# Chunk stage of a two-layer decoder step: both quarter steps behind one block, head norm weights in the rotation tables, and low halves ahead of rotations

## The chip, the cores and the metric

One core of a Trainium2 chip runs one inference step of a two-layer decoder trunk. The metric is the device time of the whole launch in microseconds, the median of three runs: 1617.29 us (1616.27 to 1617.42). The difference between two kernels is judged by medians on the same chip.

## What is computed

512 prompt tokens and 8 x 4 decode tokens (544 columns) pass two layers with shared weights for both groups. The part that the change touches is the first projection of each layer and what directly follows it for the sparse attention:

```python
a = rmsnorm(h, g_attn)
qa, ka, va, qi, ki, wi, qb, kb, vb, u = split_columns(a @ w_in)
qa = rope(rmsnorm(qa.reshape(B, T, N_HEADS_A, HEAD_DIM), g_q_a), pos)   # 6 heads of 64
ka = rope(rmsnorm(ka.reshape(B, T, N_KV_A, HEAD_DIM), g_k_a), pos)      # 2 heads of 64
qi = rope(qi.reshape(B, T, N_IDX_HEADS, IDX_DIM), pos)                  # 4 heads, no norm
ki = rope(ki[:, :, None, :], pos)[:, :, 0]
# rope: concatenate([x1*cos - x2*sin, x2*cos + x1*sin])
```

Behind it stand the selection of keys by the indexer, sparse attention, stick-breaking attention, a pooling mixer, the output projection, a convolutional FFN and a gated per-layer embedding. All of it is float32. Each large product is made from a high and a low half of both factors, three matmuls for one (`tri_product`).

## The kernel before, in words

The weights come in units of 1024 columns by 128 partitions, 106 per layer. A unit is loaded by SyncE into one of four buffers `w_raw` (`load_unit`, L519), ScalarE copies its high half to `w_H` (`split`, L892; the copy is recorded at L890) and VectorE subtracts to get its low half `w_L` (`split`, L1266, recorded at L1270). `w_H` and `w_L` have two buffers each, so the halves of unit u wait until TensorE has used unit u - 2 (`w_used`). VectorE's step raises `w_lo`, for which TensorE waits.

The chunk stage is the first in each layer. It has three chunks c (512, 452 and 384 columns of `w_in`, tokens as rows) of eight blocks k over the contraction; a unit holds two blocks, so chunk c uses the units 4c to 4c + 3. A block is four token tiles of three matmuls. The 32 decode tokens don't go through the tri-product there. `decode_step` (L1785) multiplies them in plain float32 with the unhalved weights in `w_raw`: step 0 takes the blocks 0 to 3 and stands behind k = 3, step 1 takes the blocks 4 to 7 and stands behind k = 5. The four quarters of the partitions hold partial sums, which ScalarE copies to `q_part` (`part_copy`, L980) and one matmul behind k = 7 adds (L1827). Each step raises `q_dec`. SyncE's loads of units 4 to 15 wait for it, since they overwrite what the steps read: units 4 and 5 for the first step, 6 and 7 for the second, and so on, 12 and 13 for the fifth.

From chunk 0 come the queries and keys of the sparse attention. ScalarE copies them out of PSUM with the token norm (`leave`, L960). VectorE makes the squares of the heads (`head_squares`, L1302), ScalarE the inverse roots (`inverse`), GpSimd multiplies each tile by its root (recorded at L728), waits for itself, and multiplies it by the norm weights of queries and keys (L731, L732), which raises `qk_ok`. VectorE rotates (`qk`, L1338, by `rotate`, L1315): three products with the tables of `dcon` and two additions into `r_tok` per tile, which raise `rope_ok`. TensorE transposes a tile (`turn`, L1757), ScalarE copies it to `featT` (`turned`, L952). The indexer's five heads from chunk 1 go the same way without a norm (`index` on VectorE, L1344).

The order on each engine is written out by hand, and an engine that waits holds all that stands behind it. Around the change it is:

- TensorE, c1: blocks 0 to 3, step 0, blocks 4 and 5, step 1, `turn(0, 0)`, blocks 6 and 7, sum, `turn(0, 1)`. c2: `turn(0, 2)`, `(0, 3)`, `(0, 4)`, `(1, 0)` ... `(1, 4)`, one behind each block, with the steps behind k = 3 and k = 5.
- ScalarE: split 4, `part_copy(0)`, `leave(0, 0..4)`, split 5, inverse roots, splits 6 and 7, `turned(0, 0)`, split 8, `part_copy(1)`, `turned(0, 1)`, `leave(1, 0..2)`, split 9, `turned(0, 2)`, `leave(1, 3)`, `turned(0, 3)`, `leave(1, 4)`, split 10, ..., `turned(1, 2)`, split 12, `part_copy(2)`, ...
- VectorE: split 4, `head_squares(0..2)`, split 5, `head_squares(3..4)`, split 6, `qk(0)`, split 7, `qk(1)`, split 8, `qk(2)`, `qk(3)`, split 9, `qk(4)`, `index(0)`, split 10, `index(1)`, split 11, `index(2)`, `index(3)`, split 12, `index(4)`, split 13.

Of the kernel before, what the change touches and what calls it, by code (L numbers as in the profile page):

```python
# [20 lines left out]
F32 = mybir.dt.float32  # L21
# [3 lines left out]
ALU = mybir.AluOpType  # L25
# [3 lines left out]
P = 128  # L29
# [41 lines left out]

C_ID, C_NTRI, C_NONE, C_ONE, C_INVW, C_INV16, C_EPS, C_1, C_SUM = 0, 128, 256, 384, 512, 514, 546, 547, 548
NC = 580
ACT_STEPS, DVE_STEPS, POOL_STEPS = 12, 157, 16
D_COS, D_SIN, D_MA = 0, 320, 640
ND = 928
M_REP, M_NEW = 2 * P, 4 * P
# [67 lines left out]
def build(nc, t_in, t_out):  # L145
    ctx = ExitStack()
    with ctx:
        def sb(name, shape, dt=F32, where=None):
            return (where or ctx).enter_context(nc.sbuf_tensor(name, shape, dt))
# [59 lines left out]
        raw_q = ExitStack()  # L209
        sb("raw_skip2", [P, 7336], F32, raw_q)  # L210
        q_part = sb("q_part", [P, 512], F32, raw_q)
        raw_q.close()
        stick = ExitStack()
        LW = 1280
# [151 lines left out]
        def hold(eng):  # L366


            eng.sem_inc(held, 1)
# [307 lines left out]
        def _(pool):  # L677
            for l in range(LAYERS):
# [39 lines left out]
                pool.memset(u_p[:, :, 0:15], 0.0).then_inc(u_zero, 1)  # L718
                pool.wait_ge(lay_ld, at(lay_ld, 6 * 16))
                hold(pool)  # L720
                pool.tensor_scalar(gains[:, 0, :], gains[:, 0, :], 0.125, None, ALU.mult)
                pool.wait_ge(hs_rec, at(hs_rec, 1))
                hold(pool)
                for t in range(TILES):
                    n = TOKW[t]
                    pool.wait_ge(p_ev, at(p_ev, t + 1))
                    x = x_tok[0:n, t, :].rearrange("p (h d) -> p h d", d=HD)
                    pool.tensor_tensor(x, x, hstat[0:n, t, :].unsqueeze(2).to_broadcast([n, 8, HD]), ALU.mult).then_inc(pool_step, steps.step())  # L728
                    pool.wait_ge(pool_step, steps.value())
                    hold(pool)  # L730
                    pool.tensor_tensor(x[:, 0:6, :], x[:, 0:6, :], gains[0:n, 0, :].unsqueeze(1).to_broadcast([n, 6, HD]), ALU.mult)  # L731
                    pool.tensor_tensor(x[:, 6:8, :], x[:, 6:8, :], gains[0:n, 1, :].unsqueeze(1).to_broadcast([n, 2, HD]), ALU.mult).then_inc(qk_ok, 1)  # L732
                for t in range(TILES):
                    pool.wait_ge(rope_ok, at(rope_ok, t + 1))
                    hold(pool)
# [504 lines left out]
        def _(dve):  # L1240
# [18 lines left out]
            for l in range(LAYERS):  # L1259
# [55 lines left out]
                def rotate(t, heads, parts):  # L1315

                    n = TOKW[t]
                    w = heads * HD
                    if (heads, t) != (8, 0):
                        dve.wait_ge(rope_ok, at(rope_ok, t if heads == 8 else 5 + t))  # L1320
                    x = x_tok[0:n, t, 0:w].rearrange("p (h d) -> p h d", d=HD)
                    cs = dcon[0:n, D_COS + 64 * t:D_COS + 64 * t + 64].unsqueeze(1).to_broadcast([n, heads, HD])
                    sn = dcon[0:n, D_SIN + 64 * t:D_SIN + 64 * t + 64].unsqueeze(1)
                    a = t1[0:n, 0:w].rearrange("p (h d) -> p h d", d=HD)
                    b = t2[0:n, 0:w].rearrange("p (h d) -> p h d", d=HD)
                    dve.tensor_tensor(a, x, cs, ALU.mult)
                    dve.tensor_tensor(b[:, :, 0:32], x[:, :, 32:64], sn[:, :, 0:32].to_broadcast([n, heads, 32]), ALU.mult)
                    dve.tensor_tensor(b[:, :, 32:64], x[:, :, 0:32], sn[:, :, 32:64].to_broadcast([n, heads, 32]), ALU.mult).then_inc(dve_step, steps.step())
                    dve.wait_ge(dve_step, steps.value())
                    for out, a0, a1, order in parts:  # L1330
                        i0, i1 = t1[0:n, a0:a1], t2[0:n, a0:a1]
                        if order:
                            i0, i1 = (v.rearrange("p (n j d) -> p n j d", n=2, j=3) for v in (i0, i1))
                            out = out.rearrange("p (j n d) -> p n j d", n=2, j=3)
                        ins = dve.tensor_tensor(out, i0, i1, ALU.add)
                    ins.then_inc(rope_ok, 1)

                def qk(t):  # L1338

                    n = TOKW[t]  # L1340
                    dve.wait_ge(qk_ok, at(qk_ok, t + 1))
                    rotate(t, 8, [(r_tok[0:n, t, 0:384], 0, 384, True), (r_tok[0:n, t, 384:512], 384, 512, False)])
# [67 lines left out]
                head_squares(3)  # L1410
                head_squares(4)
                split(6)
                qk(0)
                split(7)
                qk(1)
                split(8)
                qk(2)
                qk(3)
                split(9)
                qk(4)  # L1420
                index(0)
                split(10)
# [271 lines left out]
        def _(pe):  # L1694
# [12 lines left out]
            for l in range(LAYERS):  # L1707
                def at(s, n):

                    return l * per_layer[s.name] + n  # L1710
# [74 lines left out]
                def decode_step(c, step):  # L1785
# [4 lines left out]
                    elif step == 0:  # L1790
                        pe.wait_ge(p_ev, at(p_ev, i - 6))
                    if step:
                        pe.wait_ge(w_lo, at(w_lo, RAW + 4 * c + 3 + 1))
                    for j in range(4):
                        k = 4 * step + j
                        raw = w_raw[raw_slot(l, 4 * c + k // 2)]
# [4 lines left out]
                for c in range(3):  # L1801
                    w = CHUNK[c][1] - CHUNK[c][0]
                    for k in range(KD):
# [6 lines left out]
                        for t in range(TILES - 1):  # L1810
# [9 lines left out]
                            mm = tri_product(ps[0:n, i % 7, 0:w], aH[:, k, tok], aL[:, k, tok], wh, wl, k == 0, k == KD - 1)  # L1820
                            if k == KD - 1:
                                mm.then_inc(p_mm, 1)
                        if k in (3, 5):
                            decode_step(c, (k - 3) // 2)
                        if k == KD - 1:
                            pe.wait_ge(q_cp, at(q_cp, c + 1))
                            mm = pe.matmul(ps[0:TS, (5 * c + 4) % 7, 0:w], con[:, C_SUM:C_SUM + TS], q_part[:, 0:w], start=True, stop=True)  # L1827
# [4 lines left out]
                        if c == 1 and k == 1:  # L1832
# [3 lines left out]
                            for m in range(2):  # L1836
                                mm = pe.transpose(ps[:, 7, P * m:P * m + 120], pst_tok[0:120, P * m:P * m + P], ident[0:120, 0:120])
                            mm.then_inc(u_tr, 1)
                        if c == 1 and k in (5, 7):
                            turn(0, (k - 5) // 2)  # L1840
                        if c == 2:
                            turn(*((0, k + 2) if k < 3 else (1, k - 3)))

# [463 lines left out]
```

## Time and profile before

| | |
|---|---|
| median of three runs | 1617.29 us (1616.27 to 1617.42) |
| the profiled execution | 1620.47 us, its span 1618.7 us |
| mean granted clock of TensorE | 0.984 |
| TensorE busy with matmuls | 1556.1 us, 96% |
| VectorE, ScalarE, GpSimd busy | 883.4, 683.5, 276.4 us |
| chain that ended last | TensorE 79%, VectorE 13%, ScalarE 3% |
| chunk stage, first layer | about 20.9 to 105.3 us |
| chunk stage, second layer | about 812 to 897.2 us |

The page gives the shares of each engine and the chain of waits, the timelines give one instruction or a run of like ones per row. In a row of a timeline stand the start and the duration in us, the engine, the line, the operation, its output and inputs, the shape and the count, and in brackets the idle time before it with what ended that. Matmuls are pipelined, so the distance between two starts tells more of the pace than a duration.

### The profile page before, as it was taken

Reading aid. Unit: us, or ns where it says so; the run is one execution under the profiler, and the core shown is the slowest. Engines: PE = TensorE matmul, PEld = TensorE weight load, DVE = VectorE, ACT = ScalarE, POOL = GpSimd, SP = SyncE. Lnnn points to the kernel's source line nnn. Section 1 sums busy time; section 2 is a strip of 40 time slices with the busy share of each in tenths; the row PEclk is TensorE's granted clock in tenths of the full one; section 3 lists DMA queues with packets and bytes.
Section 4 is the critical chain, followed back from the end, with each engine's and each line's share of the span. In section 5 each row is a group of like instructions: output and inputs, shape, how many; then the busy total and the mean of one; then the engine's idle time right before and its main releaser. Section 6 shows DMA issues by size and latency. Waiting matters only on the chain.

```text
span 1618.7 us, 30649 instructions
## 1 busy us (share of the span) xinstructions
PE 1556.1 (96%) x11772; PEld 1415.8 (87%) x11772; DVE 883.4 (55%) x1534; ACT 683.5 (42%) x995; POOL 276.4 (17%) x474
## 2 busy tenths in 40 slices
PE   6999989999999999999999998899999999999998
PEld 5787746999999999999977776479999999999998
DVE  6668884245555553222857688624455555432345
ACT  4444556244444442224443444644444444322241
POOL 3420340111111110100115105202111111101000
PEclk8999999999999999999999999999999999999999
DMA  5233144123333233322222511332233323333221
GB/s 166 66 99 87 34 142 110 53 66 91 91 90 89 80 87 100 92 81 85 79 69 77 138 40 58 105 98 86 72 91 91 91 78 91 98 88 92 84 70 61
DMA packets 225719, 140.24 MB, mean 87 GB/s; under 512 B 13122, under 2 KB 219604, under 8 KB 225552
## 3 DMA queue, kind: packets, MB, share of 16 engines
q1 hardware_dynamic: 223220, 133.46, 28.3%
q0 software_dynamic: 2400, 5.42, 1.0%
q8 instruction: 66, 1.08, 0.3%
q14 instruction: 33, 0.27, 0.1%
HBM read 131.21 MB, written 7.65 MB: 86 GB/s over the span
## 4 chain that ended last, share of the span: by engine, by line
PE 79%; DVE 13%; ACT 3%; issue 3%; POOL 1%; DMA 0%; DVEq 0%; SPq 0%; ACTq 0%; POOLq 0%
PE ps L1714 23%; PE ps L1716 22%; PE ps L1715 22%; DVE score L1379 3%; DVE m L1376 3%; DVE w_L L1270 2%; PE ps L2065 1%; PE ps L1994 1%; DVE Lb L1451 1%; PE ps L1741 1%; PE ps L1797 1%; PE ps L1905 1%; PE ps L1767 1%; PE ps L2149 1%; PE ps L1907 1%
## 5 line engine op out<-in xcount | busy, mean ns | idle before, releaser
L1714 PE MATMUL ps<-bH,w_H 128*128 128x272 f32 x1664 | 481.1, 289 | 4.7 <-DVE w_L L1270 3.2
L1270 DVE TENSOR_TENSOR w_L<-w_raw,w_H 128x1024 fp32r<-128x1024 f32 (+4 forms) x236 | 257.6, 1100 | 414.1 <-ACT w_H L890 411.3
L1716 PE MATMUL ps<-bH,w_L 128*128 128x272 f32 x1664 | 479.6, 288 | 0.0
L1715 PE MATMUL ps<-bL,w_H 128*128 128x272 f32 x1664 | 477.9, 287 | 0.0
L890 ACT ACTIVATE w_H<-w_raw 128x1024 fp32r<-128x1024 f32 (+4 forms) x236 | 220.1, 943 | 270.1 <-PE ps L1716 269.4
L1714 PEld LDWEIGHTS ps<-bH,w_H 128*128 128x128 f32 x1664 | 312.6, 188 | 6.3 <-DVE w_L L1270 4.1
L1715 PEld LDWEIGHTS ps<-bL,w_H 128*128 128x128 f32 x1664 | 313.6, 188 | 0.1
L1716 PEld LDWEIGHTS ps<-bH,w_L 128*128 128x128 f32 x1664 | 312.6, 188 | 0.0
L1714 PE MATMUL ps<-actH,w_H 128*128 128x272 f32 x704 | 204.2, 290 | 0.0
L1716 PE MATMUL ps<-actH,w_L 128*128 128x272 f32 x704 | 203.8, 289 | 0.0
L1715 PE MATMUL ps<-actL,w_H 128*128 128x272 f32 x704 | 202.7, 288 | 0.0
L1714 PE MATMUL ps<-aH,w_H 128*128 128x272 f32 x512 | 152.7, 298 | 0.4 <-DVE u_s L1399 0.2
L1716 PE MATMUL ps<-aH,w_L 128*128 128x272 f32 x512 | 149.8, 293 | 0.0
L1715 PE MATMUL ps<-aL,w_H 128*128 128x272 f32 x512 | 149.2, 291 | 0.0
L1715 PEld LDWEIGHTS ps<-actL,w_H 128*128 128x128 f32 x704 | 132.7, 189 | 0.0
L1714 PEld LDWEIGHTS ps<-actH,w_H 128*128 128x128 f32 x704 | 132.5, 188 | 0.1
L1716 PEld LDWEIGHTS ps<-actH,w_L 128*128 128x128 f32 x704 | 132.4, 188 | 0.0
L1714 PEld LDWEIGHTS ps<-aH,w_H 128*128 128x128 f32 x512 | 98.4, 192 | 8.3 <-issue 8.2
L1715 PEld LDWEIGHTS ps<-aL,w_H 128*128 128x128 f32 x512 | 98.5, 192 | 0.0
L1716 PEld LDWEIGHTS ps<-aH,w_L 128*128 128x128 f32 x512 | 98.1, 192 | 0.0
L708 POOL TENSOR_TENSOR r_all<-r_all,a_tmp 128x544 f32<-128x544 f32 x28 | 38.0, 1356 | 295.8 <-ACT a_tmp L909 295.8
L1714 PE MATMUL ps<-w_H,aH 128*128 128x512 f32 (+2 forms) x192 | 76.1, 396 | 7.6 <-DVE aL L1282 4.9
(343 smaller groups left out, 2326.6 us busy)
## 6 DMA issues: line engine op xcount, KB each, us to landing
w_raw<-in_w_up SPq DMA_DIRECT2D x88, 512.0 KB, 3.7
w_raw<-in_w_down SPq DMA_DIRECT2D x32, 512.0 KB, 3.9
w_raw<-in_w_in SPq DMA_DIRECT2D x24, 512.0 KB, 5.0
w_raw<-in_w_ple_gate SPq DMA_DIRECT2D x16, 512.0 KB, 3.9
w_raw<-in_w_down SPq DMA_DIRECT2D x16, 384.0 KB, 3.4
w_raw<-in_w_out SPq DMA_DIRECT2D x16, 320.0 KB, 3.5
w_raw<-in_w_in SPq DMA_DIRECT2D x8, 452.0 KB, 4.0
w_raw<-in_w_in SPq DMA_DIRECT2D x8, 384.0 KB, 3.6
```

Source lines behind the costliest of these rows:

```text
L708: pool.tensor_tensor(of, of, a_tmp[:, k % 2, :], ALU.add).then_inc(n_add, 1)
L890: return act.activation(out, in_, ACT.Copy, scale=scale)
L1270: ins = dve.tensor_tensor(w_L[u % SPLIT][:, a:b], w_raw[raw_slot(l, u)][:, a:b], w_H[u % SPLIT][:, a:b].bitcast(F32), ALU.subtract)
L1376: dve.max(m8[:, :], sc).then_inc(dve_step, steps.step())
L1379: dve.match_replace(sc, m8[:, :], sc, TAKEN).then_inc(dve_step, steps.step())
L1451: dve.scalar_tensor_tensor(Lb[:, h % 2, :], Lb[:, h % 2, :], 44.0, bz_all(h), ALU.min, ALU.max).then_inc(b_max, 1)
L1714: pe.matmul(out, wh, xh, start=start, stop=False)
L1715: pe.matmul(out, wh, xl, start=False, stop=False)
L1716: return pe.matmul(out, wl, xh, start=False, stop=stop)
L1741: mm = pe.matmul(ps[:, SUM_BANK[i] + half, 0:HALF], mean, x[:, HALF * half:HALF * half + HALF], start=n == 0, stop=n == 1, skip_group_chec ...
L1767: mm = pe.transpose(ps[:, 7, P * b:P * b + n], r_tok[0:n, t, P * b:P * b + P], ident[0:n, 0:n])
L1797: mm = pe.matmul(ps[TS * j:TS * j + TS, i % 7, 0:w], xq[:, k, :], raw[:, 512 * (k % 2):512 * (k % 2) + w], start=step == 0, stop=True, ski ...
```

## The change

The quarter steps of a chunk both stand behind k = 5, and step 1 waits for the load of its last unit (`w_ld`) where it waited for that unit's low half (`w_lo`). The turns of the first two tiles move from behind k = 5 and 7 to behind k = 6 and 7. The norm weights of the heads are multiplied into copies of the cosine and sine tables, `rot_q` and `rot_k`, once per layer by GpSimd. GpSimd's work per tile is one product instead of three. VectorE's rotation of eight heads runs in two groups (six query heads, two key heads) with six smaller products for three. In VectorE's order splits 7, 8 and 9 move up by one rotation. ScalarE's and SyncE's orders are the same.

```diff
@@ gpsimd
-                pool.tensor_scalar(gains[:, 0, :], gains[:, 0, :], 0.125, None, ALU.mult)
+                pool.tensor_scalar(gains[:, 0, :], gains[:, 0, :], 0.125, None, ALU.mult).then_inc(pool_step, steps.step())
+                pool.wait_ge(pool_step, steps.value())
+                hold(pool)
+                for g, out in ((0, rot_q), (1, rot_k)):
+                    gn = gains[:, g, :].unsqueeze(1)
+                    cs, sn = (dcon[:, d:d + TILES * HD].rearrange("p (t d) -> p t d", d=HD) for d in (D_COS, D_SIN))
+                    pool.tensor_tensor(out[:, 0, :, :], cs, gn.to_broadcast([P, TILES, HD]), ALU.mult)
+                    for a in (0, 32):
+                        pool.tensor_tensor(out[:, 1, :, a:a + 32], sn[:, :, a:a + 32],
+                                           gn[:, :, 32 - a:64 - a].to_broadcast([P, TILES, 32]), ALU.mult)
...
-                    pool.tensor_tensor(x, x, hstat[0:n, t, :].unsqueeze(2).to_broadcast([n, 8, HD]), ALU.mult).then_inc(pool_step, steps.step())
-                    pool.wait_ge(pool_step, steps.value())
-                    hold(pool)
-                    pool.tensor_tensor(x[:, 0:6, :], x[:, 0:6, :], gains[0:n, 0, :].unsqueeze(1).to_broadcast([n, 6, HD]), ALU.mult)
-                    pool.tensor_tensor(x[:, 6:8, :], x[:, 6:8, :], gains[0:n, 1, :].unsqueeze(1).to_broadcast([n, 2, HD]), ALU.mult).then_inc(qk_ok, 1)
+                    pool.tensor_tensor(x, x, hstat[0:n, t, :].unsqueeze(2).to_broadcast([n, 8, HD]), ALU.mult).then_inc(qk_ok, 1)
@@ vector, rotate
+                    if heads == 8:
+                        groups = [(0, 6, rot_q[0:n, 0, t, :], rot_q[0:n, 1, t, :]), (6, 8, rot_k[0:n, 0, t, :], rot_k[0:n, 1, t, :])]
+                    else:
+                        groups = [(0, heads, *(dcon[0:n, d + 64 * t:d + 64 * t + 64] for d in (D_COS, D_SIN)))]
...
-                    dve.tensor_tensor(a, x, cs, ALU.mult)
-                    dve.tensor_tensor(b[:, :, 0:32], x[:, :, 32:64], sn[:, :, 0:32].to_broadcast([n, heads, 32]), ALU.mult)
-                    dve.tensor_tensor(b[:, :, 32:64], x[:, :, 0:32], sn[:, :, 32:64].to_broadcast([n, heads, 32]), ALU.mult).then_inc(dve_step, steps.step())
+                    for h0, h1, cs, sn in groups:
+                        m = h1 - h0
+                        cs, sn = cs.unsqueeze(1), sn.unsqueeze(1)
+                        dve.tensor_tensor(a[:, h0:h1, :], x[:, h0:h1, :], cs.to_broadcast([n, m, HD]), ALU.mult)
+                        dve.tensor_tensor(b[:, h0:h1, 0:32], x[:, h0:h1, 32:64], sn[:, :, 0:32].to_broadcast([n, m, 32]), ALU.mult)
+                        ins = dve.tensor_tensor(b[:, h0:h1, 32:64], x[:, h0:h1, 0:32], sn[:, :, 32:64].to_broadcast([n, m, 32]), ALU.mult)
+                    ins.then_inc(dve_step, steps.step())
@@ vector, order
                 split(6)
+                split(7)
                 qk(0)
-                split(7)
+                split(8)
                 qk(1)
-                split(8)
                 qk(2)
+                split(9)
                 qk(3)
-                split(9)
                 qk(4)
@@ tensor
                     if step:
-                        pe.wait_ge(w_lo, at(w_lo, RAW + 4 * c + 3 + 1))
+                        u = 4 * c + 3
+                        pe.wait_ge(w_ld[raw_slot(l, u)], ld_value(l, u))
...
-                        if k in (3, 5):
-                            decode_step(c, (k - 3) // 2)
+                        if k == 5:
+                            decode_step(c, 0)
+                            decode_step(c, 1)
...
-                        if c == 1 and k in (5, 7):
-                            turn(0, (k - 5) // 2)
+                        if c == 1 and k > 5:
+                            turn(0, k - 6)
```

## Rows read from the trace of the kernel before

**Rows 1.** Timeline of TensorE, first layer: start, duration, engine, line, operation, idle time before.

```profile
34.68 1.07 PE L1797 MATMUL ps<-w_raw,xq 128*32 128x512 f32 x8
...
45.53 1.07 PE L1797 MATMUL ps<-w_raw,xq 128*32 128x512 f32 x8
...
63.55 0.97 PE L1797 MATMUL ps<-w_raw,xq 128*32 128x452 f32 x8
64.62 0.47 PE L1714 MATMUL ps<-w_H,aH 128*128 128x452 f32 x1
...
72.75 0.96 PE L1797 MATMUL ps<-w_raw,xq 128*32 128x452 f32 x8 [2.93 <-DVE w_L L1270]
73.64 0.71 PE L1767 MATMUL ps<-con,r_tok 128*128 128x128 f32 x4
...
81.60 0.66 PE L1767 MATMUL ps<-con,r_tok 128*128 128x128 f32 x4
...
87.44 0.60 PE L1767 MATMUL ps<-con,r_tok 128*128 128x128 f32 x4
...
98.47 0.85 PE L1797 MATMUL ps<-w_raw,xq 128*32 128x384 f32 x8
...
105.00 0.37 PE L1767 MATMUL ps<-con,r_tok 32*128 32x32 f32 x3
...
131.32 1.13 PE L1894 MATMUL ps<-featT 64*128 64x512 f32 x4 [1.41 <-DVE featT L1391]
```

**Rows 2.** Timeline of TensorE, second layer.

```profile
863.48 1.74 PE L1797 MATMUL ps<-w_raw,xq 128*32 128x452 f32 x8 [2.93 <-DVE w_L L1270]
...
873.50 0.66 PE L1767 MATMUL ps<-con,r_tok 128*128 128x128 f32 x4
```

**Rows 3.** Timeline of VectorE, first layer.

```profile
33.89 1.28 DVE L1270 TENSOR_TENSOR w_L<-w_raw,w_H 128x512 fp32r<-128x512 f32 x2
...
51.12 0.69 DVE L1306 SCALAR_TENSOR_TENSOR t<-x_tok 128x512 f32<-128x512 f32 x1 [3.15 <-ACT x_tok L890]
...
62.58 1.99 DVE L1270 TENSOR_TENSOR w_L<-w_raw,w_H 128x452 fp32r<-128x452 f32 x2 [3.20 <-ACT w_H L890]
...
78.51 0.68 DVE L1326 TENSOR_TENSOR t<-x_tok,dcon 128x512 f32<-128x512 f32 x1
...
79.89 0.76 DVE L1335 TENSOR_TENSOR r_tok<-t 128x384 f32<-128x384 f32 x2
...
85.78 1.03 DVE L1270 TENSOR_TENSOR w_L<-w_raw,w_H 128x384 fp32r<-128x384 f32 x2 [2.87 <-ACT w_H L890]
...
101.31 1.23 DVE L1270 TENSOR_TENSOR w_L<-w_raw,w_H 128x1024 fp32r<-128x1024 f32 x1 [1.59 <-ACT w_H L890]
...
103.50 0.61 DVE L1335 TENSOR_TENSOR r_tok<-t 32x320 f32<-32x320 f32 x2
```

**Rows 4.** Busy time by stretch behind both waits: start:end, length, engines, granted clock.

```profile
72.70:77.50 4.80, 4.75 (x21) 3.66 (x22) 4.76 (x5) 1.85 (x4) 4.62 (x6) 0.65 0.51 162
...
863.40:869.30 5.90, 5.82 (x21) 4.00 (x22) 5.87 (x9) 1.86 (x4) 5.56 (x7) 0.50 0.42 133
```

**Rows 5.** Timeline of ScalarE, first layer: high halves of units 8, 9 and 12.

```profile
74.89 0.93 ACT L890 ACTIVATE w_H<-w_raw 128x384 fp32r<-128x384 f32 x2
...
84.77 0.98 ACT L890 ACTIVATE w_H<-w_raw 128x384 fp32r<-128x384 f32 x2
...
100.23 1.05 ACT L890 ACTIVATE w_H<-w_raw 128x1024 fp32r<-128x1024 f32 x1
```

**Rows 6.** Timeline of GpSimd, first layer: the norm weights of the queries, first tile.

```profile
62.69 1.39 POOL L731 TENSOR_TENSOR x_tok<-x_tok,gains 128x384 f32<-128x384 f32 x1 [0.18 <-POOL x_tok L728]
```

**Rows 7.** DMA issues, the loads issued at 46.79 and 93.76: KB, us to landing.

```profile
w_raw<-in_w_in SPq DMA_DIRECT2D x1, 452.0 KB, 3.3
...
w_raw<-in_w_in SPq DMA_DIRECT2D x1, 512.0 KB, 3.8
```

**Rows 8.** Timeline of SyncE's queue: the issue of the load of unit 6.

```profile
46.79 0.37 SPq L560 DMA_DIRECT2D w_raw<-in_w_in  x1
```

More of the change, by code:

```diff
@@ L73 @@
 NC = 580
-ACT_STEPS, DVE_STEPS, POOL_STEPS = 12, 157, 16
+ACT_STEPS, DVE_STEPS, POOL_STEPS = 12, 157, 12
 D_COS, D_SIN, D_MA = 0, 320, 640
@@ L211, in build @@
         q_part = sb("q_part", [P, 512], F32, raw_q)
+        rot_q = sb("rot_q", [P, 2, TILES, HD], F32, raw_q)
+        rot_k = sb("rot_k", [P, 2, TILES, HD], F32, raw_q)
         raw_q.close()
@@ L1321, in rotate @@
                     x = x_tok[0:n, t, 0:w].rearrange("p (h d) -> p h d", d=HD)
-                    cs = dcon[0:n, D_COS + 64 * t:D_COS + 64 * t + 64].unsqueeze(1).to_broadcast([n, heads, HD])
-                    sn = dcon[0:n, D_SIN + 64 * t:D_SIN + 64 * t + 64].unsqueeze(1)
+                    if heads == 8:
+                        groups = [(0, 6, rot_q[0:n, 0, t, :], rot_q[0:n, 1, t, :]), (6, 8, rot_k[0:n, 0, t, :], rot_k[0:n, 1, t, :])]
+                    else:
+                        groups = [(0, heads, *(dcon[0:n, d + 64 * t:d + 64 * t + 64] for d in (D_COS, D_SIN)))]
                     a = t1[0:n, 0:w].rearrange("p (h d) -> p h d", d=HD)
                     b = t2[0:n, 0:w].rearrange("p (h d) -> p h d", d=HD)
-                    dve.tensor_tensor(a, x, cs, ALU.mult)
-                    dve.tensor_tensor(b[:, :, 0:32], x[:, :, 32:64], sn[:, :, 0:32].to_broadcast([n, heads, 32]), ALU.mult)
-                    dve.tensor_tensor(b[:, :, 32:64], x[:, :, 0:32], sn[:, :, 32:64].to_broadcast([n, heads, 32]), ALU.mult).then_inc(dve_step, steps.step())
+                    for h0, h1, cs, sn in groups:
[5 more added lines that the diff above has]
+                    ins.then_inc(dve_step, steps.step())
                     dve.wait_ge(dve_step, steps.value())
```

## Prediction

> **What bounds the kernel now.** I read the page first. Its row of engines has TensorE busy for nearly the whole span and its chain of waits runs mostly over the tri-product matmuls, so a change counts by what it does to TensorE's idle time and clock. Then I read the waits of TensorE in the chunk stage, then the timelines of TensorE, VectorE, ScalarE, GpSimd and the load queue there, in both layers. I call a layer's three chunks c0, c1, c2, their eight blocks k0 to k7, and write "quarter step" for `decode_step`.
>
> TensorE has one long wait in this stage: behind k5 of c1 it stands 2.93 us before quarter step 1, released by the VectorE subtraction that makes the low half of unit 7; the second layer has the same wait of 2.93 us [rows 1, 2]. That subtraction stood on VectorE behind `qk(0)`, and `qk(0)` behind GpSimd's three products per tile. While GpSimd multiplies, VectorE is slow: a 452-column low half took 1.99 us for its two pieces, where a 384-column one took 1.03 us without GpSimd [rows 3]. Then the clock falls: the granted clock of the stretch behind the wait is 0.65, a mean over 2.4 and 1.2 GHz, and 0.50, all 1.2 GHz, in the second layer [rows 4]. From quarter step 1 to `turn(0, 1)` it took 8.85 us in the first layer and 10.02 us in the second [rows 1, 2]. At full clock the same work is 1.0 for the step, 0.4 for the transposes, two blocks of 2.5 and, as for a step, 0.9 for the sum over quarters, about 7.25 us in all (the blocks from the step of 64.62 to the end of the idle time at 72.75: 8.13 less 2.93 is 5.2 for two with their drain) [rows 1]. So slow clock costs 1.6 and 2.8 us.
>
> **What the change removes.** Both waits and both slow stretches: 2.93 + 1.6 = 4.5 us in the first layer, 2.93 + 2.8 = 5.7 in the second, 10.2 together. The weights' gains leave GpSimd's two products per tile and go into four table blocks, written while GpSimd has nothing to do between the layer's loads and the head statistics. They are off the path; their price is what they slow on VectorE. They are six products with 1280 elements per partition in all, against 384 in 1.39 us [rows 6], so some 4 to 5 us beside the low halves of units 2 and 3. Unit 3 has 8 us to spare, unit 2 is below.
>
> **What it adds, point by point.** The removed wait covered nothing, but the moved instructions did, and what stands behind them on each queue decides.
>
> (a) c0, k4. Quarter step 0 ran from 34.68 to about 35.7 and hid the end of unit 2's low half, 33.89 + 1.28 = 35.17 [rows 1, 3]. With the step gone, TensorE waits from 34.68 to about 35.3, 0.6 us (bounds 0.5 and, with that subtraction at half pace, 1.3). In the second layer it is between nothing and the same; I take nothing, as there the blocks ahead of it don't follow a cold start.
>
> (b) c1, k4. SyncE may load units 4 and 5 only on `q_dec`, which step 0 raises; that step now stands behind k5. In the first layer it ends at about 46.2 (before, step 1 began at 45.53 with 1.07 us [rows 1]; less the 0.99 of the removed step, plus the 0.6 of (a), plus 1.07). The load is issued 0.2 later (46.60 to 46.79) and lands 3.3 after that [rows 1, 7, 8], at 49.7. ScalarE's queue has that high half ahead of the copy of the quarters and of the first `leave(0, t)`: 49.8 + 1.0 = 50.8, and VectorE's low half of unit 4, 1.1 us, stands ahead of `head_squares(0)`, which so starts at about 52.15 instead of 51.12 [rows 3]. From there to the low half of unit 6 everything waits in one line (five head squares, ScalarE's inverse root, high half of 6, low half of 6), so that ends at 64.57 + 1.05 = 65.6 [rows 3]. Before, TensorE began k4 at 64.62, right behind it, with step 0 (from 63.55) in the gap [rows 1]. Now TensorE is there at 63.55 + 0.6 = 64.15 and waits 1.5 us. k4 begins 1.05 late in the first layer, 0.45 late in the second, where (a) doesn't delay the load. Units 6 and 7 are issued behind the same two steps, in time.
>
> (c) c1, `turn(0, 1)`. `turn(0, 0)` moves from behind k5 to behind k6. ScalarE's order isn't changed: `turned(0, 0)` stands ahead of the high half of unit 8. VectorE's is: the low half of unit 8 now stands ahead of `qk(1)`. So `qk(1)`, which had been done by then, waits for TensorE's `turn(0, 0)`. From its start: 2.1 to the end of the high half (73.64 to 74.89 + 0.93 is 2.18 at the low clock), 1.0 for the low half, 2.3 for `qk(1)`: 5.4 us [rows 1, 3, 5]. A `qk` ran 2.14 from 78.51 to 79.89 + 0.76 [rows 3]; with six smaller products for three it has three more fixed parts, for which I take 0.2 (bounds 0 and 0.5). TensorE wants `turn(0, 1)` after 0.4 + 2.5 + 0.9 = 3.85 us. Wait: 1.55.
>
> (d) c2, `turn(0, 3)`. The low half of unit 9 now stands ahead of `qk(3)`. Before, VectorE had `qk(3)` done and then idled 2.87 us for that high half [rows 3]. From `turn(0, 1)`: 84.77 + 0.98 - 81.60 = 4.15 to the high half's end, 1.0 for the low half, 2.3 for `qk(3)`, 7.45 us. TensorE wants it after 87.44 - 81.60 = 5.84 [rows 1, 5]. Wait: 1.6.
>
> (e) c2, `turn(1, 4)`. Units 12 and 13 load on step 0 of c2, now behind k5. From the end of k5: step 0.85, issue 0.2, landing 3.8, high half 0.1 + 1.05, low half 1.28 with its release, `index(4)` 1.6 (102.5 to 103.50 + 0.61), 8.9 us [rows 1, 3, 5, 7]. TensorE wants its turn after 105.00 - 98.47 = 6.53 plus 0.8 for the second step beside it, 7.35. Wait: 1.55 (bounds 1.0 and 2.5 for landings of 3.3 and 4.8).
>
> **The sum**, against the profiled run's own 1620.47. First layer: k4 of c1 at 64.62 + 1.05 = 65.67; two blocks 5.05, two steps 2.0, k6 2.5 give `turn(0, 0)` at 75.2; plus 5.4 is `turn(0, 1)` at 80.65 (before 81.60, so 0.95 early). To the end of k5 of c2 it was 98.47 - 81.60 = 16.87; less a step of 0.8, plus (d) 1.6, is 17.67: 98.3. Plus 8.9 is `turn(1, 4)` at 107.2, where it had been 105.00: 2.2 late. Second layer: the same stretch starts 0.6 less late, and before it lost 1.2 us more to the clock (10.02 against 8.85): 0.4 late. Together 2.6 us slower with the clock kept. What follows (features, then the selection on VectorE and the stick stage) starts from there on every engine, so nothing takes it back. A weight load waits for nothing but these units, and the cache loads wait on the rotations.
>
> **The clock.** It fell after 2.93 us of idle TensorE twice [rows 1, 2, 4] and did not after 1.41 us, behind which matmuls of 512 columns ran at full pace, four in 1.13 us [rows 1]. My eight waits of 1.5 to 1.6 lie between, close to the one that cost nothing, but those of (c) and (e) stand beside thin work (32-row sums, transposes). A fall costs about 1.6 us. One behind (c) costs little, since it also makes TensorE later at (d). I count one that isn't absorbed: 4.2 us. Measured runs lie 3.2 below the profiled one, before and after alike I assume: 1617.3 + 4.2 = 1621.5.
>
> The Trainium skill (TensorE: Matmul & The Clock Gate, "What's actually happening") has the array at half rate by default and once it has been idle, and at full rate after sustained work. Taken strictly, none of these short waits would cost clock. By that rule the trace agrees only in part: the clock fell behind a wait of 2.93 us with work on both sides of it [rows 1, 4].
>
> **The rivals.** First, the gain as meant, the other side. If the low halves of 8, 9 and 12 come early enough that the turns find their rotations (this decides at 1.5 us of slack each: ScalarE would have to be through the high half that much sooner), only (a) and (b) are left. Then `turn(0, 1)` is 0.95 + 1.55 = 2.5 early in the first layer, 2.75 + 1.55 = 4.3 in the second: 6.8 us faster, 1610.5. For it: GpSimd's freed time. Against it: high half 8 waits for a transposition that TensorE itself does later now. Chance 0.10. Second, all waits as computed and no clock fall, as behind the wait of 1.41 [rows 1]: 2.6 us, 1619.9. Chance 0.27. Third, waits half as long, because two adjacent quarter steps and earlier landings give time back: 3 us less than the second, 1617. Chance 0.11. Fourth, three or more falls: 2.6 + 5, 1625. Chance 0.12. The forecast, one or two falls, 1620.9 to 1623.5: 0.40.
>
> **How the numbers follow.** A measurement of this kernel tells about 0.2%, 3.2 us, from no change: 1614.1 and 1620.5 are the borders. Faster: the first rival, 0.10. Within: the third, three quarters of the second, 0.32 with a rest of the forecast's lower edge. Slower: 0.58. The range leaves out the first rival and half of the fourth: 1615.5 to 1626. The forecast alone reaches from 1620.5 to 1624.
>
> **What would show it.** In the changed trace: no wait before the quarter steps; a wait of some 1.5 us at k4 of c1 released by VectorE's subtraction; waits at `turn(0, 1)`, `turn(0, 3)` and `turn(1, 4)` released by VectorE's additions into `r_tok`; `head_squares(0)` about a microsecond later; loads of 12 and 13 issued at about 99.4; GpSimd's products in the c1 stretch less than half as many. If the turns show no waits, (c) to (e) are wrong and the first rival holds. If they do and the granted clock is full throughout, it is the second.

## The result and the profile after

The changed kernel took 1627.18 us in the median (1626.55 to 1628.28, four runs) against 1616.97 us for the kernel before (four runs). The ratio is 1.0064 with a 95% interval of 1.0047 to 1.0082, so it is slower by 8 to 13 us. Run again with a later set of kernels it took 1627.66 us against 1616.23, ratio 1.0065 (1.0044 to 1.0087). The sign was forecast, the size was not: 4.2 us were predicted, the range ended at 1626.

TensorE's waits in the first layer's chunk stage, longest in total first (engine, line, releaser, then total, count, longest). The first row is the wait at which the stage starts, which is there before the change too (4.92 us in both). Line numbers are those of the changed kernel.

```profile
PE ps L1727 <- DVE aL L1289: 4.9, 1, 4.9
PE ps L1780 <- DVE r_tok L1348: 4.9, 3, 1.7
PE ps L1727 <- DVE w_L L1277: 3.2, 2, 2.4
PE ps L1727 <- ACT x_tok L897: 0.3, 1, 0.3
```

The wait of 2.93 us before quarter step 1 [rows 1] is gone. In its place stand five: two for a low half and three for the additions that end a rotation. The timeline of TensorE in the first layer shows each at its place.

```profile
34.85 0.47 PE L1727 MATMUL ps<-w_H,aH 128*128 128x512 f32 x1 [0.86 <-DVE w_L L1277]
...
65.95 0.57 PE L1727 MATMUL ps<-w_H,aH 128*128 128x452 f32 x1 [2.36 <-DVE w_L L1277]
67.07 0.58 PE L1727 MATMUL ps<-w_H,aH 128*128 128x452 f32 x1
...
70.08 0.37 PE L1727 MATMUL ps<-w_H,aH 128*128 128x452 f32 x1
...
72.64 1.72 PE L1811 MATMUL ps<-w_raw,xq 128*32 128x452 f32 x16
...
82.39 0.63 PE L1780 MATMUL ps<-con,r_tok 128*128 128x128 f32 x4 [1.60 <-DVE r_tok L1348]
...
90.00 0.63 PE L1780 MATMUL ps<-con,r_tok 128*128 128x128 f32 x4 [1.62 <-DVE r_tok L1348]
...
109.06 0.34 PE L1780 MATMUL ps<-con,r_tok 32*128 32x32 f32 x3 [1.68 <-DVE r_tok L1348]
109.33 0.40 PE L1727 MATMUL ps<-aH,w_H 128*128 128x272 f32 x1
```

They are (a) to (e) of the prediction: block 4 of chunk 0, block 4 of chunk 1, `turn(0, 1)`, `turn(0, 3)` and `turn(1, 4)`. Both quarter steps now run without a wait, sixteen matmuls in one row. The matmuls behind the wait at 65.95 stand 1.12 us apart for three and last 0.58 us; from 70.08 on they last 0.37. The second layer has the same waits but the first:

```profile
862.05 0.48 PE L1727 MATMUL ps<-w_H,aH 128*128 128x452 f32 x1 [2.27 <-DVE w_L L1277]
...
876.94 0.63 PE L1780 MATMUL ps<-con,r_tok 128*128 128x128 f32 x4 [1.61 <-DVE r_tok L1348]
...
884.55 0.63 PE L1780 MATMUL ps<-con,r_tok 128*128 128x128 f32 x4 [1.61 <-DVE r_tok L1348]
...
903.83 0.34 PE L1780 MATMUL ps<-con,r_tok 32*128 32x32 f32 x3 [1.72 <-DVE r_tok L1348]
```

VectorE in the first layer, the rows that answer to rows 3: low half of unit 4, first head square, low halves of units 6 and 7 in one row of four pieces, then the low halves of units 8, 9 and 12.

```profile
50.49 1.17 DVE L1277 TENSOR_TENSOR w_L<-w_raw,w_H 128x452 fp32r<-128x452 f32 x2 [13.57 <-ACT w_H L897]
51.63 0.69 DVE L1313 SCALAR_TENSOR_TENSOR t<-x_tok 128x512 f32<-128x512 f32 x1
...
63.09 5.57 DVE L1277 TENSOR_TENSOR w_L<-w_raw,w_H 128x452 fp32r<-128x452 f32 x4 [3.20 <-ACT w_H L897]
...
78.95 1.03 DVE L1277 TENSOR_TENSOR w_L<-w_raw,w_H 128x384 fp32r<-128x384 f32 x2 [8.01 <-ACT w_H L897]
...
86.55 1.03 DVE L1277 TENSOR_TENSOR w_L<-w_raw,w_H 128x384 fp32r<-128x384 f32 x2 [1.84 <-ACT w_H L897]
...
106.11 1.23 DVE L1277 TENSOR_TENSOR w_L<-w_raw,w_H 128x1024 fp32r<-128x1024 f32 x1 [4.75 <-ACT w_H L897]
```

VectorE stands idle for 8 us ahead of the low half of unit 8. `qk(1)` was ready to run behind it, since GpSimd had all five tiles done by 68.2. One product per tile is all that is left of GpSimd's work in rows 6:

```profile
61.98 6.20 POOL L739 TENSOR_TENSOR x_tok<-x_tok,hstat 128x512 f32<-128x512 f32 x5 [22.88 <-ACT hstat L922]
```

ScalarE tells why the high halves come late. Twice, for units 4 and 12, it waits for a load that SyncE could not issue earlier. The high half of unit 8 stands behind the copy of `turn(0, 0)`, for which ScalarE waits 12.76 us on TensorE. At `leave(1, 3)` it waits for a rotation.

```profile
49.41 1.05 ACT L897 ACTIVATE w_H<-w_raw 128x452 fp32r<-128x452 f32 x2 [4.43 <-DMA w_raw<-in_w_in]
...
77.50 0.60 ACT L897 ACTIVATE featT<-ps 128x512 f32<-128x512 f32 x1 [12.76 <-PE ps L1780]
77.99 0.93 ACT L897 ACTIVATE w_H<-w_raw 128x384 fp32r<-128x384 f32 x2
...
89.89 0.53 ACT L897 ACTIVATE x_tok<-ps,r_col 128x324 f32<-128x324 f32 x1 [2.62 <-DVE r_tok L1348]
...
105.02 1.06 ACT L897 ACTIVATE w_H<-w_raw 128x1024 fp32r<-128x1024 f32 x1 [2.39 <-DMA w_raw<-in_w_in]
```

Where the time went between the two profiled executions, from the starts of TensorE's first matmul of chunk 0 and of its first matmul of the feature stage (us). "The chunk stage" below is always this stretch. It is the best measure of a place in what follows, since whole runs of one kernel lie up to 3 to 7 us from their median. It holds for one execution of each kernel, with the falls of the clock that this execution happened to have.

| stretch | before | after | more |
|---|---|---|---|
| up to the first layer's chunk stage | 20.94 | 20.49 | -0.45 |
| chunk stage, first layer | 84.36 | 88.84 | 4.48 |
| between | 706.80 | 708.49 | 1.69 |
| chunk stage, second layer | 85.10 | 86.27 | 1.17 |
| rest | 721.49 | 722.42 | 0.93 |
| span | 1618.7 | 1626.5 | 7.8 |

### The profile page after: what moved, and what is told of

It reads as the page before. It is cut to its first block, busy times and chain, and to the rows that moved or that the text cites. A ratio compares the mean times of both kernels' runs of the same rounds, so it can differ in the third digit from the quotient of the medians.

```text
span 1626.5 us, 30663 instructions
## 1 busy us (share of the span) xinstructions
PE 1552.7 (95%) x11772; PEld 1414.3 (87%) x11772; DVE 876.5 (54%) x1564; ACT 683.1 (42%) x995; POOL 266.8 (16%) x466
## 4 chain that ended last, share of the span: by engine, by line
PE 77%; DVE 13%; ACT 4%; issue 4%; DMA 1%; SPq 0%; DVEq 0%; POOL 0%; ACTq 0%; POOLq 0%
PE ps L1727 22%; PE ps L1729 22%; PE ps L1728 22%; DVE score L1392 3%; DVE m L1389 2%; DVE w_L L1277 2%; PE ps L2080 1%; ACT w_H L897 1%; DMA w_raw<-in_w_in 1%; DVE aL L1289 1%; PE ps L2009 1%; DVE Lb L1464 1%; PE ps L1754 1%; PE ps L1920 1%; PE ps L2164 1%
## 5 line engine op out<-in xcount | busy, mean ns | idle before, releaser
L1277 DVE TENSOR_TENSOR w_L<-w_raw,w_H 128x1024 fp32r<-128x1024 f32 (+4 forms) x236 | 261.1, 1116 | 433.8 <-ACT w_H L897 431.0
L1728 PEld LDWEIGHTS ps<-aL,w_H 128*128 128x128 f32 x512 | 99.4, 194 | 0.0
```

Source lines behind the costliest of these rows:

```text
L1277: ins = dve.tensor_tensor(w_L[u % SPLIT][:, a:b], w_raw[raw_slot(l, u)][:, a:b], w_H[u % SPLIT][:, a:b].bitcast(F32), ALU.subtract)
L1728: pe.matmul(out, wh, xl, start=False, stop=False)
```

## The experiments

The column "ratio" is against the kernel before, run beside it. "Stage" is the sum of both layers' chunk stages in the profiled execution; it was 169.5 us before and 175.1 us after.

| kernel | median, us | before, us | ratio (95%) | stage, us |
|---|---|---|---|---|
| changed, again | 1627.66 | 1616.23 | 1.0065 (1.0044 to 1.0087) | 175.3 |
| e1, changed, order of before | 1621.27 | 1618.13 | 1.0013 (0.9998 to 1.0029) | 167.1 |
| e2, changed, places of before | 1611.91 | 1618.13 | 0.9960 (0.9943 to 0.9976) | 165.7 |
| e3, changed, both of before | 1611.45 | 1618.13 | 0.9959 (0.9945 to 0.9974) | 160.6 |
| e4, changed, GpSimd later | 1620.07 | 1618.13 | 1.0009 (0.9997 to 1.0020) | 172.8 |
| e5, before, wait for the load | 1611.58 | 1617.17 | 0.9960 (0.9945 to 0.9975) | 162.5 |
| e6, before, tables | 1611.67 | 1617.17 | 0.9965 (0.9954 to 0.9977) | 160.9 |
| e7, changed, steps of chunk 2 as before | 1621.26 | 1617.17 | 1.0031 (1.0015 to 1.0046) | 170.6 |
| e8, e3 and an early high half 6 | 1608.24 | 1617.17 | 0.9952 (0.9931 to 0.9972) | 158.7 |
| e9, changed, early high half 6 | 1620.64 | 1616.23 | 1.0023 (1.0009 to 1.0037) | 168.6 |
| e10, e5 and an early high half 6 | 1614.73 | 1616.23 | 0.9997 (0.9979 to 1.0015) | 165.7 |

My theory was that of the prediction: each moved instruction delays what stands behind it on its queue. The first rival was that the order costs nothing and the smaller rotations and the fuller GpSimd cost the time.

**e1, the order of the low halves.** VectorE's order as before, all else changed.

```diff
                 split(6)
-                split(7)
                 qk(0)
-                split(8)
+                split(7)
                 qk(1)
+                split(8)
                 qk(2)
-                split(9)
                 qk(3)
+                split(9)
                 qk(4)
```

> The changed kernel with VectorE's order of before (low half 7 behind qk(0), 8 behind qk(1), 9 behind qk(3)), all else as changed. Theory: the waits of 1.6 us at turn(0, 1) and turn(0, 3) come from the low halves put ahead of qk(1) and qk(3). Both vanish in both layers, those at block 4 of chunk 1 (2.3) and at turn(1, 4) (1.7) stay: 6.4 us less than the changed kernel, about 1621, or 4 us above before. Rival (the six small products and the fuller GpSimd cost the time, the order nothing): the turns wait all the same and the time stays at 1627.

The stage is 8.0 us shorter than the changed kernel's: 6.4 for the four waits, and the clock did not fall inside the stage here where it had fallen behind the wait at 65.95. The ratio went from 1.0064 to 1.0013. Waits of TensorE, first layer:

```profile
PE ps L1727 <- DVE w_L L1277: 4.1, 2, 2.5
PE ps L1780 <- DVE r_tok L1348: 1.7, 1, 1.7
PE ps L1727 <- ACT x_tok L897: 0.3, 1, 0.3
```

Of three waits on a rotation one is left, that at `turn(1, 4)`. (c) and (d) come from the low halves put ahead of `qk(1)` and `qk(3)`.

**e2, the places of the steps and turns.** Steps behind blocks 3 and 5, turns behind 5 and 7, all else changed.

```diff
-                        if k == 5:
-                            decode_step(c, 0)
-                            decode_step(c, 1)
+                        if k in (3, 5):
+                            decode_step(c, (k - 3) // 2)
...
-                        if c == 1 and k > 5:
-                            turn(0, k - 6)
+                        if c == 1 and k in (5, 7):
+                            turn(0, (k - 5) // 2)
```

> The changed kernel with the quarter steps behind blocks 3 and 5 and the turns behind 5 and 7, as before; VectorE's order, tables and the wait for the load stay changed. Theory: the loads of units 4, 5, 12 and 13 start a block or two earlier, so the waits at block 4 of chunk 1 (all but some 0.8 of it, since low half 6 is still slowed by GpSimd) and at turn(1, 4) vanish, the wait at turn(0, 1) too, as turn(0, 0) comes a block earlier; the one at turn(0, 3) stays, 1.6 per layer. About 10 us removed of before and 5 us left: 1611 to 1613. Rival (place of the steps is free, the order alone costs): turn(0, 1) and turn(1, 4) still wait, 1623 to 1627.

1611.91 us, and the waits are those expected:

```profile
PE ps L1780 <- DVE r_tok L1348: 1.6, 1, 1.6
PE ps L1727 <- DVE w_L L1277: 0.9, 1, 0.9
PE ps L1727 <- ACT x_tok L897: 0.3, 1, 0.3
```

With the turn of the first tile a block earlier, (c) goes even in the changed order. So (c) needs both edits, (d) the order alone, (e) the places alone.

**e3, both back.** The edits of e1 and e2 together.

> The changed kernel with both the order and the places of before; only the tables and the wait for the load are left of the change. Theory: the 2.93 us wait and the fall of the clock go and nothing comes in their place but up to 0.8 us at block 4 of chunk 1: 1607 to 1610, 7 to 10 us below before. Rival (the removed waits reappear at block 6, which needs low half 7 anyway): that wait is 1 to 2 us in each layer and the time is 1613 to 1616.

1611.45 us, 0.41% faster than before, with the stage 8.9 us shorter than before. The wait of 2.93 us didn't come back at block 6. The only wait of the low halves is at block 4 of chunk 1:

```profile
63.16 0.47 PE L1727 MATMUL ps<-w_H,aH 128*128 128x452 f32 x1 [0.93 <-DVE w_L L1277]
```

The whole time fell by 6.7 us, a little under the 7 to 10 expected, and isn't told apart from e2's, though e2 keeps a wait of 1.6 us per layer and its stage is 5.1 us longer, 3.2 of it these waits and the rest mostly a fall of the clock in chunk 0 (granted clock 0.50 from 41 to 44 us).

**e4, GpSimd's products later.** They start only when the low half of unit 6 has been made.

```diff
                 pool.wait_ge(hs_rec, at(hs_rec, 1))
+                pool.wait_ge(w_lo, at(w_lo, RAW + 6 + 1))
                 hold(pool)
```

> The changed kernel with GpSimd's products of the five tiles held until low half 6 is done. Theory: low half 6 took 2 x 1.46 us because GpSimd multiplied without a pause beside it; alone it takes 2 x 0.63, so the wait at block 4 of chunk 1 falls from 2.3 to about 0.7 us in both layers and with it the fall of the clock behind it in the first layer: 3.3 to 5 us less, 1622 to 1624. The other waits stay. Rival (the length of that wait is set by the late load of unit 4 alone): low half 6 and the wait stay as they are, 1627.

TensorE, VectorE and GpSimd at block 4 of chunk 1:

```profile
64.28 0.48 PE L1728 MATMUL ps<-w_H,aH 128*128 128x452 f32 x1 [0.83 <-DVE w_L L1278]
```

```profile
63.05 1.17 DVE L1278 TENSOR_TENSOR w_L<-w_raw,w_H 128x452 fp32r<-128x452 f32 x2 [3.20 <-ACT w_H L898]
```

```profile
64.39 6.25 POOL L740 TENSOR_TENSOR x_tok<-x_tok,hstat 128x512 f32<-128x512 f32 x5 [25.46 <-DVE w_L L1278]
```

The low half took 1.17 us for its two pieces and the wait fell from 2.36 to 0.83 us (0.89 in the second layer). The line of VectorE's subtractions alone (count, then the least, median and longest duration in ns) shows what it had been, first for the changed kernel (units 6 and 7), then for the kernel before (unit 6):

```profile
L1277 DVE TENSOR_TENSOR w_L<-w_raw,w_H x4: 1415/1462/1464, 63.1 to 67.2; 128x452 fp32r<-128x452 f32 x4
```

```profile
L1270 DVE TENSOR_TENSOR w_L<-w_raw,w_H x2: 630/1036/1442, 62.6 to 63.1; 128x452 fp32r<-128x452 f32 x2
```

Before, GpSimd paused for 0.18 us behind its first product while it waited for itself. The first piece began in that pause (62.58) and took 0.63 us, the second began beside the next product and took 1.44. With one product per tile, five in a row, there is no such pause and both pieces take over 1.4 us (2.80 together). The last section comes back to this.

The rest of the wait, 0.83, is what the later load and the step that no longer stands in the gap leave. The time is 1620.07 us, 7.1 below the changed kernel where 3.3 to 5 were expected. The stage accounts for 2.3 of it. Two different sets of runs are compared there, and what makes up the rest was not tested.

**e5, the wait for the load alone.** The kernel before with one edit.

```diff
                     if step:
-                        pe.wait_ge(w_lo, at(w_lo, RAW + 4 * c + 3 + 1))
+                        u = 4 * c + 3
+                        pe.wait_ge(w_ld[raw_slot(l, u)], ld_value(l, u))
```

> The kernel before with only one edit: quarter step 1 waits for the load of its last unit, not for that unit's low half. Theory: block 6 needs the same low half, and GpSimd and qk(0) still stand ahead of it, so the wait of 2.93 us moves behind the step and one transposition: 1.5 to 1.7 us at block 6 of chunk 1 in both layers. 1.3 us less per layer, and 1.5 to 3 more per layer if the clock no longer falls: 3 to 8 us below before. Rival (the wait for the low half was the whole cost): no wait left, 8 to 10 us below before.

The wait moved to block 6 and halved, as the theory has it, and this time the clock did not fall behind it:

```profile
71.79 0.47 PE L1714 MATMUL ps<-w_H,aH 128*128 128x452 f32 x1 [1.45 <-DVE w_L L1270]
```

1611.58 us, 5.6 below before. The step and the turn are work that now runs while the low half is made, so 1.5 us of the wait is left.

**e6, the tables alone.** The kernel before with the tables and the small rotations; the wait for the low half stays.

> The kernel before with only the tables (GpSimd one product per tile, VectorE six small products per rotation of eight heads); steps, turns, order and the wait for the low half as before. Theory: GpSimd is done some 9 us sooner and low half 7 is ready when quarter step 1 comes to it, so the 2.93 us wait goes without the other edits; left is 0.8 to 0.9 at block 4 of chunk 1. Same as the kernel that also has the wait for the load: 6 to 9 us below before. Rival (the wait for the load is what counts): a wait over 1 us stays before quarter step 1, 2 to 4 us below before.

The step has no wait, though it still asks for the low half: `qk(0)` is through at about 68.5 and the low half of unit 7, made behind it without GpSimd beside it, took 1.16 us. Left is

```profile
64.67 0.47 PE L1727 MATMUL ps<-w_H,aH 128*128 128x452 f32 x1 [0.93 <-DVE w_L L1277]
```

Stage 160.9, time 1611.67, the same as e3; 5.5 us below before, where 6 to 9 were expected. So each of two edits of the change brings some 5.5 us without the other: the tables take the wait away, the wait for the load halves it. Together (e3) they bring little more than one alone. The other two edits, the order and the places, only cost.

**e7, the steps of chunk 2.** The changed kernel with only chunk 2's steps back.

```diff
-                        if k == 5:
+                        if c < 2 and k == 5:
                             decode_step(c, 0)
                             decode_step(c, 1)
+                        if c == 2 and k in (3, 5):
+                            decode_step(c, (k - 3) // 2)
```

> The changed kernel with the quarter steps of chunk 2 alone back behind blocks 3 and 5. Theory: the loads of units 12 and 13 start two blocks sooner, so low half 12 and index(4) are in time and the wait of 1.7 us at turn(1, 4) vanishes in both layers, as does the clock's fall behind it; all other waits stay. 3.4 to 6.6 us below the changed kernel. Rival (turn(1, 4) waits because index(4) itself is late, behind qk(3) and qk(4)): the wait stays.

```profile
PE ps L1727 <- DVE w_L L1277: 3.9, 2, 2.4
PE ps L1780 <- DVE r_tok L1348: 3.2, 2, 1.6
PE ps L1727 <- ACT x_tok L897: 0.3, 1, 0.3
```

The wait at `turn(1, 4)` is gone, the two others on rotations stay. (e) is the load of unit 12, not a late `index(4)` of itself. The stage is 4.5 us shorter. The two waits are 3.4 of it, the fall of the clock behind (b), which this execution doesn't have, some 1.7, and the wait (a) was 0.6 longer here. The ratio went from 1.0064 to 1.0031.

**e9, the high half of unit 6 early.** The changed kernel with ScalarE's split 6 ahead of the inverse roots.

```diff
                 split(5)
+                split(6)
                 act.wait_ge(hs_ss, at(hs_ss, 1))
                 inverse(hstat[:, :, :], hstat[:, :, :]).then_inc(hs_rec, 1)
...
                 ins.then_inc(ph_ev, 1)
-                split(6)
                 split(7)
```

> The changed kernel with ScalarE's high half of unit 6 ahead of the inverse roots. Theory: low half 6 is made before GpSimd's products start, so its pieces take 0.63 us and not 1.46, and the wait at block 4 of chunk 1 goes altogether (it was 2.3 us); the three waits at the turns stay. 4.6 us below the changed kernel, up to 3 more for the fall behind it: 1619 to 1623. Rival (the wait comes from the late load of unit 4 and only shrinks by the high half's place): over 0.8 us stays.

VectorE makes that low half right behind the last head square, ahead of GpSimd's products:

```profile
58.67 1.15 DVE L1277 TENSOR_TENSOR w_L<-w_raw,w_H 128x452 fp32r<-128x452 f32 x2
```

(b) is gone in both layers, the three waits at the turns stay at 4.9 us per layer, the time is 1620.64, 7.0 below the changed kernel beside it.

**e8, the best of these.** e3 with the same early high half.

> The kernel with only the tables and the wait for the load, and in addition ScalarE makes the high half of unit 6 ahead of the inverse roots. Theory: low half 6 is then made before GpSimd starts its products and the last 0.9 us wait at block 4 of chunk 1 goes: 1.8 us below the kernel without this, 8 to 11 below before. Rival (ScalarE's inverse roots come later by 1 us and so do the rotations): a new wait at the turns takes it back.

1608.24 us, 0.48% below before (0.28 to 0.69%), faster than both kernels. Between the start of the chunk stage and the features the first layer's TensorE has two short waits left, 0.28 us for a low half at block 4 of chunk 0 and one for a copy of ScalarE:

```profile
76.17 0.44 PE L1727 MATMUL ps<-w_H,aH 128*128 128x384 f32 x1 [0.32 <-ACT x_tok L897]
```

The stage is 1.9 us shorter than e3's, 79.32 against 80.29 in the first layer and 79.35 against 80.29 in the second, for 1.8 expected. The wait of 0.93 at block 4 of chunk 1 is gone in both layers and no turn waits, so the rival is out. In the whole time the lead over e3 is not settled: the intervals of the two ratios overlap.

**e10, the early high half without the tables.** e5 with the edit of e9.

> The kernel before with the wait for the load and the early high half of unit 6, without the tables: GpSimd makes three products per tile. Theory: low half 6 is out of GpSimd's way, but low half 7 stands behind qk(0), which waits for GpSimd's three products of the first tile, so the wait at block 6 of 1.5 us stays or grows by what GpSimd starts later: 1.4 to 2.0 us, 5 to 8 us below before. Rival (GpSimd's products are not what holds qk(0) and low half 7): the wait goes and the time equals that with the tables and the early high half.

The wait at block 6 stayed, and another came at `turn(0, 0)`:

```profile
70.24 0.63 PE L1767 MATMUL ps<-con,r_tok 128*128 128x128 f32 x4 [0.88 <-DVE r_tok L1335]
...
72.34 0.47 PE L1714 MATMUL ps<-w_H,aH 128*128 128x452 f32 x1 [1.46 <-DVE w_L L1270]
```

No gain that the interval shows, 1614.73 against 1616.23, where 5 to 8 us were expected. Two things were left out. In e5, as before, block 4 of chunk 1 has no wait that an earlier low half 6 could take away. And the high half of unit 6 now stands ahead of the inverse roots, so `qk(0)` and the low half of unit 7 come 0.8 us later in the second layer, counted from the start of its stage, and TensorE 0.2 sooner. The two waits together are 2.3 us per layer, where 1.4 to 2.0 were expected. In the first layer the clock fell behind them (0.50 from 73 to 76 us). The wait stayed as the theory had it, its size and the time were missed.

**The changed kernel again.**

> The changed kernel itself, on the chip of the next two. Where the clock falls moves from run to run, so the theory (waits of fixed length, falls that come and go) expects the same waits to 0.1 us in the trace, 2.3, 1.6, 1.6 and 1.7 us per layer, and falls at one to four of them; the time 7 to 10 us above before. Rival (the first comparison was off by more than the falls): waits of other lengths, or a difference under 5 us.

Its waits in both layers are those of the first look, 2.37 for the low half and 4.9 in three for rotations. The time is 11.4 us above the median of before, 10.5 by the ratio, a little over the 7 to 10 expected. Its falls are not those of the first look: none behind block 4 of chunk 1 in either layer, one behind `turn(1, 4)` in each, and one at 41.3 us in chunk 0, beside the sums of the token norm, where the first look had none.

## Why the prediction was right and wrong

**What is removed.** Right. The wait and both slow stretches behind it went [rows 1, 2, 4]. e3, which keeps the removal and puts the rest back, has stages 8.9 us shorter with a new wait of 0.93 in each, so the 10.2 were right for the profiled execution. That either the tables or the wait for the load alone brings most of it (e6, e5) was not foreseen.

**(a)** 0.6 was computed, 0.86 us measured in the first layer (0.8 to 1.6 in the variants, where the upper bound was 1.3) and nothing in the second, as taken.

**(b)** This is the term of the sum that was mis-sized: 1.5 us in each layer, and it measured 2.36 and 2.27. The load landed 3.4 us after its issue at 45.97 and the head squares began at 51.63. Counted from the start of the stage, which was 0.45 us earlier in this execution, both they and TensorE's arrival were within 0.1 us of the working. The error is the last link: I let the low half of unit 6 take 1.99 us as in rows 3. It took 2.8. The prediction had counted on GpSimd's slowing of VectorE as before, and did not ask what taking away two of three products does to the pauses between them. Two runs show it. With GpSimd held back (e4) the low half took 1.17 us and the wait is 0.83 and 0.89. With the tables as the only edit (e6) the low half took 2.81, and block 4 waits 0.93 where it had not waited before. The miss is about 0.8 us per layer.

**(c), (d), (e)** Right in place, releaser and size: 1.60, 1.62 and 1.68 us for 1.55, 1.6 and 1.55. e1 and e7 take them away one by one. The `qk` of six small products ran 79.89 to 82.25, 2.36 us, for 2.3. The load of unit 12 went out at 101.17, not at 99.4, as TensorE was late by then, and landed 3.85 us later. The new wait in `leave(1, 3)` on ScalarE (2.62 us) was not in the working; no wait of TensorE goes back to it.

**The sum.** It had 2.2 us for the first layer and 0.4 for the second, with the clock kept. The chunk stages grew by 4.5 and 1.2. In the second layer the difference of 0.8 is (b). In the first it is 2.3: 0.9 from (b) and 1.7 from a fall of the clock behind (b), less a rest of 0.3. No fall was priced at that place, because the wait was to be short.

**The clock.** One fall was counted. The granted clock behind (b) and behind `turn(1, 4)` in the first layer, and behind (b) in the second (start:end, length, engines, clock):

```profile
66.20:69.60 3.40, 3.40 (x10) 2.98 (x10) 3.40 (x6) 0.00 (x0) 1.98 (x2) 0.50 0.00 0
...
110.60:114.00 3.40, 3.40 (x18) 3.40 (x17) 1.23 (x1) 2.34 (x5) 2.44 (x5) 0.50 0.51 169
```

```profile
862.00:865.40 3.40, 3.35 (x16) 3.08 (x17) 3.40 (x4) 0.00 (x0) 2.28 (x2) 1.00 0.02 5
```

Two falls, each some 3.4 us at half clock and so some 1.7 us of time, and none behind the wait of 2.27 in the second layer. The second fall lies behind the stage, in the stretch "between", which grew by 1.69. In the changed kernel's second run the stretch behind the same wait of 2.4 in the first layer kept its clock, but both turns were followed by a fall:

```profile
64.00:70.00 6.00, 3.63 (x19) 2.98 (x18) 6.00 (x6) 1.05 (x2) 5.03 (x4) 1.00 0.00 0
```

```profile
904.00:908.00 4.00, 4.00 (x24) 4.00 (x23) 1.22 (x1) 3.23 (x6) 2.48 (x5) 0.63 0.40 125
```

So a wait of this length is followed by a fall in some executions and not in others, and a wait of 1.68 us at `turn(1, 4)` was followed by one. What decides it these runs don't show. The second rival (no fall at all) was wrong. By the count of falls the forecast's own case, one or two, held in the profiled execution; the fourth rival (three or more, 1625) is nearest to the measured time, but only because (b) and the next point come on top. The rule of the Trainium skill (TensorE: Matmul & The Clock Gate, "What's actually happening"), which has the array at half rate once it has been idle, taken strictly would have allowed none behind such short waits; the falls behind 2.36 and 1.68 us go against that.

**From the profiled run to the median.** This was the largest miss. I assumed that measured runs lie 3.2 us below the profiled one for both kernels. For the changed kernel it was 1.1. The spans differ by 7.8 us, the medians by 10.2. The profiled execution of before had a mean granted clock of 0.984. Of the 68 executions of before beside the experiments, the eight with that clock took 1618.5 to 1621.6 us, the ten with 0.989 took 1613.3 to 1617.3. The four executions of the changed kernel all had 0.986 or 0.987. So the profiled execution of before was one of those with much slow clock, and the 4.4 us of slow clock that the working counted as gained are more than the median execution had to give. e3 and e6 point the same way: stages 8.9 and 8.6 us shorter than that execution's, medians only 6.7 and 5.5 lower.

Of the 6.0 us by which 4.2 fell short of 10.2, 2.4 is this assumption, 1.6 is (b) and some 1.7 a second fall. The 0.3 that remains is not explained. In it lies what the first stretch of the table lost (0.45) and the last one gained (0.93).

**The first rival**, the gain as meant, fell: the turns waited. But e3 shows that the gain it described exists once the order and the places are put back.

## What to carry to other kernels

Before an instruction is moved up an in-order queue, read what it waits for at its new place: a low half ahead of a rotation is only early if its high half is, and that one hung on a transposition which the same change had put later. A small step between two long ones may be cover and the trigger of a load at once; moved behind its neighbour it gives up both. And when one engine's work is cut to a third, what is left may run without pauses and slow a neighbour more than before, so price the neighbour's work at its slowest rate. Slow clock that one profiled execution shows is no gain to count in full before other executions have been looked at.

## What the runs showed of the hardware that was not expected

VectorE's subtraction of 452 columns from two buffers took 0.63 us alone and up to 1.46 us where GpSimd multiplied, 2.3 times as long. What it took in between follows from when it began. GpSimd and VectorE in the changed kernel, then in e9:

```profile
62.98 1.04 POOL L739 TENSOR_TENSOR x_tok<-x_tok,hstat 128x512 f32<-128x512 f32 x1
63.09 1.42 DVE L1277 TENSOR_TENSOR w_L<-w_raw,w_H 128x452 fp32r<-128x452 f32 x1 [3.20 <-ACT w_H L897]
```

```profile
62.80 1.05 POOL L739 TENSOR_TENSOR x_tok<-x_tok,hstat 128x512 f32<-128x512 f32 x1
63.61 0.73 DVE L1277 TENSOR_TENSOR w_L<-w_raw,w_H 128x452 fp32r<-128x452 f32 x1 [3.80 <-ACT w_H L897]
```

Both pieces end 0.49 us after the end of the product that ran when they began (64.51 for 64.02, 64.34 for 63.85). The second piece of before ends 0.48 us after it (63.12 to 64.56, product to 64.08), the first piece of unit 7 in e4 0.49 (64.63 to 65.92, product to 65.43). A piece that began while GpSimd paused took its 0.63 us though the next product came beside it (62.58 before). So the price of an overlap depends on how much of GpSimd's product is still to run when VectorE begins, and the pause of 0.18 us saved 0.8 here.

The granted clock fell behind waits of 1.68 and 2.36 us and stayed full behind waits of 2.27 and 2.37 us at the same place as the latter. In e10 it fell behind two waits of 0.88 and 1.46 us in the first layer and stayed behind the same two in the second.
